# Expert rows of PEER gathered and summed in packs of 4 picks by 32 tokens, product-key search two heads at a time, a new table of ticks

## The reference

```python
scores = jnp.einsum('thpd,hpnd->thpn', qry, sub_keys).astype(jnp.float32)
top_s, top_i = lax.top_k(scores, PEER_TOPK)
cand_s = top_s[:, :, 0, :, None] + top_s[:, :, 1, None, :]
cand_i = top_i[:, :, 0, :, None] * PEER_NKEYS + top_i[:, :, 1, None, :]
...
best_s, best_pos = lax.top_k(cand_s, PEER_TOPK)
idx = jnp.take_along_axis(cand_i, best_pos, axis=-1)
gate = jax.nn.softmax(best_s, axis=-1)
u = expert_u[idx]
act = jax.nn.gelu(jnp.einsum('thkd,td->thk', u, x_blk), approximate=False)
vsel = expert_v[idx]
return jnp.einsum('thk,thkd->td', (gate * act).astype(vsel.dtype), vsel)
```

## Time and profile before

| | |
|---|---|
| median of 3 runs | 1902.19 us |
| span of the profiled execution, first to last instruction | 1833.1 us |
| what lies around the span (median less span) | 69.1 us |
| TensorE busy | 1408.6 us (77%) |
| VectorE busy | 1011.9 us (55%) |
| GpSimd busy | 1096.8 us (60%) |
| ScalarE busy | 400.6 us (22%) |
| bytes moved by DMA | 619.35 MB, mean 338 GB/s |

### The profile page before, as it was taken

The page is one execution under the profiler, slowest core; times in us unless marked ns, Lnnn a source line. Parts: engine busy times, 40 slices in busy tenths (PEclk is TensorE's granted clock), DMA queues, the critical chain, the costliest instruction groups (busy, mean ns, idle before and its releaser), DMA issues.

```text
span 1833.1 us, 14206 instructions
## 1 busy us (share of the span) xinstructions
PE 1408.6 (77%) x4217; PEld 708.3 (39%) x4217; DVE 1011.9 (55%) x2342; ACT 400.6 (22%) x1019; POOL 1096.8 (60%) x1049
## 2 busy tenths in 40 slices
PE   7988405776887896697868878867899977778886
PEld 6768402222332332245423333323564433223332
DVE  4655697774544444864595456477308355444441
ACT  5645201111211211520112102133213202111111
POOL 2010038777777675776656777557535677777772
PEclk9999757989999898898889898979999988998898
DMA  8250239999999999999988999999978899999995
GB/s 324 80 207 1 84 133 332 389 361 383 409 409 409 366 383 402 409 397 404 404 309 302 409 409 405 401 405 329 397 248 276 318 391 401 389 410 409 409 409 202
DMA packets 182515, 619.35 MB, mean 338 GB/s; under 512 B 18405, under 2 KB 18441, under 8 KB 182441
## 3 DMA queue, kind: packets, MB, share of 16 engines
q0 software_dynamic: 153568, 561.12, 79.5%
q1 hardware_dynamic: 28496, 57.28, 8.3%
q10 hardware_dynamic: 376, 0.05, 0.0%
HBM read 617.34 MB, written 1.05 MB: 337 GB/s over the span
## 4 chain that ended last, share of the span: by engine, by line
PE 30%; DMA 24%; POOL 24%; DVE 11%; issue 9%; ACT 2%; ACTq 0%; DVEq 0%
PE banks L492 19%; POOL arena L308 18%; DMA arena<-in_peer_u_dram,hnT 12%; POOL raw L308 6%; DMA arena<-in_peer_v_dram,hnT 6%; DMA raw<-in_peer_u_dram,hnT 5%; PE banks L370 3%; PE banks L376 3%; DVE arena L1309 2%; PE banks L630 1%; DVE arena L1353 1%; DVE arena L1351 1%; PE banks L516 1%; DVE raw L1309 1%; DMA arena<-in_diff_w_in_dram 1%
## 5 line engine op out<-in xcount | busy, mean ns | idle before, releaser
L492 PE MATMUL banks<-arena,hnT 128*128 128x512 f32 x2048 | 1024.7, 650 | 324.9 <-ACT hnT L851 267.8
L492 PEld LDWEIGHTS banks<-arena,hnT 128*128 128x128 f32 x2048 | 408.5, 207 | 887.5 <-issue 562.7
L308 POOL DMA_INDIRECT arena<-in_peer_v_dram,hnT x512 | 535.6, 1046 | 250.4 <-PE banks L492 143.0
L1309 DVE CUSTOM_DVE_ANT_0 raw<-raw,hrows 128x1024 f32<-128x1024 f32 x256 | 312.4, 1224 | 313.6 <-DMA raw<-in_peer_u_dram,hnT 312.6
L1309 DVE CUSTOM_DVE_ANT_0 arena<-arena,hrows 128x1024 f32<-128x1024 f32 x256 | 311.7, 1224 | 274.6 <-DMA arena<-in_peer_u_dram,hnT 274.2
L308 POOL DMA_INDIRECT raw<-in_peer_u_dram,hnT x256 | 273.1, 1067 | 255.2 <-DVE hnT L1409 140.6
L308 POOL DMA_INDIRECT arena<-in_peer_u_dram,hnT x256 | 274.3, 1071 | 110.0 <-issue 70.4
L851 ACT ACTIVATE hnT<-ident,hnT 128x128 f32<-128x128 f32 x512 | 169.7, 391 | 159.2 <-PE banks L492 119.0
L845 ACT ACTIVATE hnT<-hnT 128x8 f32<-128x8 f32 x64 | 13.4, 209 | 810.8 <-DVE hnT L1309 810.7
L516 PE MATMUL banks<-arena,work 128*128 128x512 f32 x256 | 124.3, 621 | 12.5 <-ACT work L873 6.8
L1041 DVE TENSOR_TENSOR split<-arena,split 128x512 fp32r<-128x512 f32 x96 | 63.5, 689 | 47.6 <-ACT split L716 47.2
(11 more groups left out here) (194 smaller groups left out, 708.9 us busy)
## 6 DMA issues: line engine op xcount, KB each, us to landing
arena<-in_diff_w_in_dram SPq DMA_DIRECT2D x24, 1024.0 KB, 18.1
arena<-in_peer_w_query_dram SPq DMA_DIRECT2D x16, 1024.0 KB, 13.4
arena<-in_gla_w_in_dram POOLq DMA_DIRECT2D x5, 2048.0 KB, 23.0
arena<-in_peer_w_query_dram POOLq DMA_DIRECT2D x4, 2048.0 KB, 16.6
arena<-in_peer_v_dram,hnT POOLq DMA_INDIRECT x512, 7.8
arena<-in_diff_w_out_dram SPq DMA_DIRECT2D x8, 1024.0 KB, 19.7
arena<-in_gla_w_out_dram POOLq DMA_DIRECT2D x2, 2048.0 KB, 10.9
raw<-in_peer_u_dram,hnT POOLq DMA_INDIRECT x256, 7.9
```

Of the source, the lines that this page charges most:

```text
L308: pool.indirect_dma_start(rows(n), None, table.rearrange("l e d -> (l e) d"), bass.IndirectOffsetOnAxis(ap=places[:, o:o + 1].bitcast(u32) ...
L492: last = nc.tensor.matmul(bank(2 * (tile % NT) + half), diags[:, n % BUFS * P:(n % BUFS + 1) * P], v_rows(n)[:, half * 512:(half + 1) * 51 ...
L1309: V.tensor_tensor_reduce(out=u_rows(n), in0=u_rows(n), in1=hrows[:, o // SLOTS, :], scale=1.0, scalar=0.0, op0=ALU.mult, op1=ALU.add, accu ...
```

## The change

Five things, in one diff.

1. **V rows in packs.** A V gather of before brings, for one pick, the rows of 128 tokens. Now four V gathers together bring four picks of 128 tokens in another arrangement: gather j of a pack brings the rows of tokens 32j to 32j+31, and the partition's quarter says which of the four picks it is. The number of gathers and their size stay. The list of places, the gates and the Gelus have to be rearranged for that, which ScalarE does in 16 small copies each (`packed`, on 32 partitions): per list of 32 picks for places and gates, per 8 picks for the Gelu.
2. **Sums of 32 columns.** The weight matrix of a gather is 128x32 (four stacked identities, `ident4`, scaled), and its sum writes 32 partitions of PSUM: `expert_sums` does eight matmuls of 128x32 by 128x512 for a pack of four, four next to each other into the four quarters of a bank. V buffers come free in fours.
3. **Search and lists per two heads.** `search(tile, b)` handles heads 2b and 2b+1 and sets `listed` for 32 picks; the softmax of these two heads is part of it. The order on DVE beside it is changed: between the lists of tile 2 stand steps of layer 1 of the second token group.
4. **A new table.** From tick 16 on one U and one V gather per tick, V 16 picks behind U, to tick 520 (before: 598 ticks). `START` is now 0, 128, 256, 384, `BASE` 148 and 276.
5. Key scores of layer 1 are computed block by block within the query projection, so that the first search can start earlier (`SEARCH_T` is counted from `Q_END[0]`).

```diff
+PACK = 4
+LIST = 2 * TOPK
+LISTS = SLOTS // LIST
+PACK_T = P // PACK
...
+LAG = 16
+PLAN = ((0, 0, 0), (LAG, LAG, 0), (ROWS, ROWS, ROWS - LAG), (ROWS + LAG // 2, ROWS, ROWS))
 TICKS = PLAN[-1][0]
-START = (0, 128, 280, 464)
-GATES = (0, 55, 268, 450)
-BASE = (140, 326)
-FINAL = 492
+START = (0, 128, 256, 384)
+BASE = (148, 276)
+FINAL = 430
...
-SEARCH_T = Q_END[3] + 4
+SEARCH_T, PAIR_T = Q_END[0] + 4, 15
+SEARCH = [PAIR_T * n for n in range(NT * LISTS)] + [t + SEARCH_T + PAIR_T * b for t in BASE for b in range(LISTS)]
+SEARCH[10], SEARCH[11] = BASE[1] + 2, BASE[1] + IN_END[1] + 2
...
                 for n in range(v_at(t), v_at(t + 1)):
+                    if n % LIST == 0:
+                        pool.wait_ge(S("v_listed"), n // LIST + 1)
                     if n >= BUFS:
-                        pool.wait_ge(S("v_used"), n - BUFS + 1)
-                    gather(peer_v, n, v_rows, "v_loaded")
+                        pool.wait_ge(S("v_used"), (n - BUFS) // PACK + 1)
+                    gather(peer_v, n, v_places, v_rows, "v_loaded")
...
-            def expert_sum(n):
-
-                tile = n // SLOTS
-                if n % SLOTS == 0 and tile >= NT:
+            def expert_sums(first):
+
+                tile = first // SLOTS
+                if first % SLOTS == 0 and tile >= NT:
                     pe.wait_ge(S("h_updated"), 2 * (tile - NT + 1))
-                pe.wait_ge(S("diag_ready"), n + 1)
-                pe.wait_ge(S(f"v_loaded{n % BUFS}"), 16 * (n // BUFS + 1))
+                pe.wait_ge(S("diag_ready"), first + PACK)
+                for n in range(first, first + PACK):
+                    pe.wait_ge(S(f"v_loaded{n % BUFS}"), 16 * (n // BUFS + 1))
                 for half in range(2):
-                    last = nc.tensor.matmul(bank(2 * (tile % NT) + half),
-                                            diags[:, n % BUFS * P:(n % BUFS + 1) * P],
-                                            v_rows(n)[:, half * 512:(half + 1) * 512],
-                                            start=(n % SLOTS == 0), stop=(n % SLOTS == SLOTS - 1))
+                    for j in range(PACK):
+                        n, r0 = first + j, j * PACK_T
+                        last = nc.tensor.matmul(bank(2 * (tile % NT) + half)[r0:r0 + PACK_T, :],
+                                                diags[:, n % BUFS * PACK_T:(n % BUFS + 1) * PACK_T],
+                                                v_rows(n)[:, half * 512:(half + 1) * 512],
+                                                start=(first % SLOTS == 0), stop=(first % SLOTS == SLOTS - PACK))
                 last.then_inc(S("v_used"), 1)
...
-                while summed < v_at(int(t) - SUM_LAG):
-                    expert_sum(summed)
-                    summed += 1
+                while summed + PACK <= v_at(int(t) - SUM_LAG):
+                    expert_sums(summed)
+                    summed += PACK
...
+            def packed(dst, src, function):
+
+                for s in range(PACK):
+                    to = dst[s * PACK_T:(s + 1) * PACK_T].rearrange("p (g j) -> p g j", j=PACK)
+                    for j in range(PACK):
+                        of = src[j * PACK_T:(j + 1) * PACK_T].rearrange("p (g s) -> p g s", s=PACK)
+                        last = A(to[:, :, j], of[:, :, s], function)
+                return last
...
-                A(acts[:, o], dots[:, o], ACT.Gelu).then_inc(S("gelu_done"), 1)
+                packed(acts[:, o], dots[:, o], ACT.Gelu).then_inc(S("gelu_done"), 1)
...
-                A(diags[:, n % BUFS * P:(n % BUFS + 1) * P], ident[:], ACT.Copy,
+                A(diags[:, n % BUFS * PACK_T:(n % BUFS + 1) * PACK_T], ident4[:], ACT.Copy,
                   scale=weights[:, n % PICKS:n % PICKS + 1]).then_inc(S("diag_ready"), 1)
...
-                two_rounds(HP, 350, lambda j: sc[:, j * NK:(j + 1) * NK],
+                two_rounds(4, 260, lambda j: sc[:, j * NK:(j + 1) * NK],
...
+            attended(0)
+            search(2, 0)
+            search(2, 1)
+            mix_rows(1)
+            search(2, 2)
+            turned(1, 0)
+            search(2, 3)
+            turned(1, 1)
+            attended(1)
+            for b in range(LISTS):
+                search(3, b)
```

More of the change, by code:

```diff
@@ L61, with lists_at @@
 Q_END = [Q_T + 4 * KD * Q_STEP * (b + 1) for b in range(4)]
-SEARCH_T = Q_END[3] + 4
+SEARCH_T, PAIR_T = Q_END[0] + 4, 15
+SEARCH = [PAIR_T * n for n in range(NT * LISTS)] + [t + SEARCH_T + PAIR_T * b for t in BASE for b in range(LISTS)]
+SEARCH[10], SEARCH[11] = BASE[1] + 2, BASE[1] + IN_END[1] + 2
+def lists_at(t, late, after):
+    return sum(min(SEARCH[n] + late, START[n // LISTS] + n % LISTS * LIST + after) <= t
+               for n in range(2 * NT * LISTS))
 def placed(t, which):
@@ L176, in trunk_kernel @@
         words = hnT[:].rearrange("p k t -> p (k t)")
-        dots, acts, weights, places, diags = (words[:, o:o + n] for o, n in (
-            (0, PICKS), (PICKS, PICKS), (2 * PICKS, PICKS), (3 * PICKS, PICKS), (4 * PICKS, BUFS * P)))
+        dots, acts, weights, places, v_places, gates, diags = (words[:, o:o + n] for o, n in (
+            (0, PICKS), (PICKS, PICKS), (2 * PICKS, PICKS), (3 * PICKS, PICKS), (4 * PICKS, PICKS),
+            (5 * PICKS, PICKS), (6 * PICKS, BUFS * PACK_T)))
         def x1(unit, off=0, n=D):
@@ L304, in _, with gather @@
                                    ).then_inc(S("keys_loaded"), 16)
-            def gather(table, n, rows, loaded):
+            def gather(table, n, of, rows, loaded):
                 o = n % PICKS
@@ L1331, in at, with tops, search @@
                     ticks += 1
-            def tops(off, half):
-                return ar(off, HP * TOPK).rearrange("p (h q k) -> p h q k", h=PH, q=2)[:, :, half, :]
-            def search(tile, t):
+            def tops(off, half, b):
+                return ar(off + b * 4 * TOPK, 4 * TOPK).rearrange("p (h q k) -> p h q k", h=2, q=2)[:, :, half, :]
+            def search(tile, b):
+                t = SEARCH[tile * LISTS + b]
+                at(t)
+                first = tile % NT * SLOTS + b * LIST
                 spent = 0
-                latest = START[tile]
+                latest = START[tile] + b * LIST
                 def used(ns):
@@ L1373, in search @@
+                step(V.tensor_copy(ar(tif, 4 * TOPK), ar(ti, 4 * TOPK).bitcast(u32)))
+                s1 = tops(A_TS, 0, b).unsqueeze(3).broadcast_to([P, 2, TOPK, TOPK])
+                s2 = tops(A_TS, 1, b).unsqueeze(2).broadcast_to([P, 2, TOPK, TOPK])
+                step(V.tensor_tensor(cand.rearrange("p (h a b) -> p h a b", h=2, a=TOPK), s1, s2, ALU.add))
+                used(800)
                 ordered()
-                bs, bp, gg = A_BS, A_BP, A_GG + tile % NT * SLOTS
-                two_rounds(PH, 480, lambda j: cand[:, j * 256:(j + 1) * 256],
+                bs, bp, gg = A_BS + b * LIST, A_BP + b * LIST, A_GG + first
@@ L1405, in search @@
-                    used(2300)
+                    step(V.tensor_reduce(ar(ij + half * LIST, LIST), e3, AX.X, ALU.add))
+                    used(600)
                 ordered()
-                step(V.tensor_scalar(ar(ij, SLOTS), ar(ij, SLOTS), float(NK), float(tile // NT * NEXP), ALU.mult, ALU.add))
+                step(V.tensor_scalar(ar(ij, LIST), ar(ij, LIST), float(NK), float(tile // NT * NEXP), ALU.mult, ALU.add))
                 ordered()
-                V.tensor_tensor(places[:, tile % NT * SLOTS:(tile % NT + 1) * SLOTS].bitcast(i32), ar(ij, SLOTS), ar(ij + SLOTS, SLOTS),
+                V.tensor_tensor(places[:, first:first + LIST].bitcast(i32), ar(ij, LIST), ar(ij + LIST, LIST),
@@ L1410, in search @@
                                 ALU.add).then_inc(S("listed"), 1)
[L1412 to L1416 removed]
+                sm = A_SM
+                dve.wait_ge(S("gate_exps"), tile * LISTS + b + 1)
+                step(V.tensor_reduce(ar(sm, 2), g3, AX.X, ALU.add))
```

193 lines of the change are left out of this document (101 added, 92 removed).

## The result

The changed kernel takes **1977.85 us**, the median of 4 runs (1971.25 to 1985.16), where the kernel before took 1901.68 us beside it: ratio **1.0395 [1.0361, 1.043]**. It is slower; 1821 us and a gain had been forecast. The profiled execution took 1977.94 us.

The account below looks back on a forecast made before the run. No engine was taken to bound the whole; the second half was a flow of gathers with a floor of 1.28 us each. 1626 + 33 + 5 + 30 + 12 = 1706, + 45.7 = 1752, with 69.1 gives 1821 us; range 1760 to 1890.

Parts of the forecast that it names:

- The first U gather: Start of the gather flow: a quarter of the search suffices, so it starts at 214.2 us, 40 us earlier (38 to 42).
- the rival: TensorE's 32-column sums: the columns don't overlap, a pack takes 6.9 us, 1866 us in all; chance 0.07.
- The search's 0.10 us for each gather: Search beside the dots on VectorE: lengthens each of 330 gathers by 0.10 us, 33 us in all (0 to 115).
- The sum: Whole kernel: last U gather at 1706 us plus 45.7 us of end gives 1752 us of span, 81 less than before.
- the floor: Whole kernel: dots and gathers fall into step, attention has slack, only 12 us of waits remain; 1753 us; chance 0.15.
- ScalarE. ... Nothing is added to the sum: ScalarE's Gelus of 16 instructions take 3.3 us for 0.2, 64 times; V 16 ticks behind U covers it, cost 0.
- Outside layer 1 ... no stall: V buffers outside layer 1: rows land after 7.8 us, sum 2 us, buffer needed 12.8 us behind; no stall.
- V buffers in packs: Attention of layer 1: loop of 14.0 us against 10.2, 3.8 us for each of 4 packs, twice: 30 us (0 to 60).
- half clock: TensorE: granted clock falls towards 0.50, a pack takes 4 us in 10.2; it waits for nothing there, costed at nothing.
- In the projections the weights fill such gaps: Projections of layer 1: weight loads fill the gaps from V buffer waits; hardly any waits of GpSimd for sums expected there.
- fourth rival: All of layer 1: GpSimd goes in step with TensorE, 3.8 us for each of 45 packs, 1962 us; chance 0.09.
- the 69.1 us around the span: Outside the profiled span: 69.1 us taken as time around it, added to 1752 us of span to give 1821 us.

## Why the prediction was wrong

**What held.** The first U gather starts at 214.6 us (214.2 had been worked out); its wait is ended by the first list:

```profile
L1467 DVE TENSOR_TENSOR hnT<-arena x16: 191/192/193, 214.2 to 1664.9; 128x32 int32<-128x32 f32 x16
```

Four sums of 32 columns do run side by side. At the full clock a pack is 1.92 us, where 2.0 was said and 6.9 would have been the rival. The first row stands behind an idle stretch, at a mean granted clock of 0.55, the second right behind it, at 1.00:

```profile
1612.49 3.41 PE L509 MATMUL banks<-arena,hnT 128*32 128x512 f32 x16 [17.96 <-issue]
1617.25 1.92 PE L509 MATMUL banks<-arena,hnT 128*32 128x512 f32 x16 [1.35 <-DMA arena<-in_peer_v_dram,hnT]
```

The Trainium skill (TensorEngine Tiling (Array Packing), Theoretical Speedup) gives up to 4x for 32 columns; the second row shows 6.9 / 1.92 = 3.6, and the earlier trace rows had shown only two. The search's 0.10 us for each gather is neither borne out nor refuted. With the diagonals first, 8 ticks took 21.8 us with the search beside them (picks 16 to 120), but 22.7 in the last flow without it; with SUM_LAG 2 as well they took 22.6 and 21.1. What lengthens a gather there is a dot, search or none, and the sum had counted that for the ticks with a search only. In the changed kernel itself a gather took 1.57 us in those ticks, above the 1.5 that the prediction named as a sign against it. The sum, 1752 us of span, is nearly met by the kernel without packs (1742.7), which is not the kernel it was made for, and by that with both edits (1765.0). The range began at 1760 us, above the 1753 of the floor that it was said to nearly take in.

**The step that failed first** is "ScalarE. ... Nothing is added to the sum", with its cover of 16 ticks. The 3.3 us were right (3.44). Wrong was to look at how far V stands behind U and not at what stands ahead of what in ScalarE's queue in one tick. With 16 = 2 x 8 the late Gelu and the needed diagonal meet in every group. The order of ScalarE's instructions that is shown ahead of the prediction says it: two Gelus, then seven diagonals (L898, x7) and not eight. The eighth, without which the second pack isn't whole, stands behind the third Gelu. I read there only that each Gelu had become 16 instructions. The same holds for "Outside layer 1 ... no stall": the V buffers were counted to be needed 12.8 us behind the gather, with the sum ready as soon as rows and TensorE were, and no diagonal in the count. Price on chip A: 136 us (147 by the ratios), the gain of the diagonals put first. The sentence "If the cover were gone, a pack's diagonals would be 3.3 us late and so would the V gathers" had the mechanism: 8 ticks were 25.4 - 22.7 = 2.7 us longer for it in the last flow, and over some 60 groups that is 160 us, less what loads hide.

**The step that was too small** is "V buffers in packs". For the attention it had "14.0 us where the flow needs 10.2" (its terms add up to 13.9), 4 packs, twice, 30 us. The loop is there as described, with 17.6 us in place of 14.0 and 5 or 6 packs a pass. The largest part of the error is the pack, taken at 2 us: it was written three paragraphs before that TensorE would fall to half clock and that this costs nothing, and exactly here TensorE is waited for. It is 3.64 us. With SUM_LAG 2 the loop has room again, and 68 us are gained with the diagonals first (40 of the 79 us between the two profiled spans lie in the attentions). That this lock comes of freeing V buffers in fours is shown by the kernel without packs that waits in fours. Wrong outright was "In the projections the weights fill such gaps": the fours cost 55 us in the parts of layer 1 outside the attentions, and the changed kernel waits 40.2 us for sums in one input projection alone. So the prediction's fourth rival, GpSimd in step with TensorE through all of layer 1, to which it gave 0.09, was right in its place, though not in its price. It is half of the story: against the kernel without packs on A the changed kernel loses 109 us in layer 1 (U picks 148 to 375: 840.7 and 732.0 us), but also 63 us ahead of it and 57 behind it, where the Gelu holds the diagonal.

**The step beside them** is "the 69.1 us around the span": no run has more than some 2 us there. Chip A and chip B differ by 3.3% for before (1840.81 and 1901.68 us), and by 0.1% for the changed kernel. This hid part of the error: on chip A the ratio is 1.081.

**The sum.** On chip A, from the changed kernel: 1980.17 - 136.4 (diagonals first) - 67.7 (SUM_LAG 2) = 1776.1 us, which is simply the time of the kernel with both, against 1752 + 2 forecast for a chip like it. Its profiled span is 1765.0 us: the last U gather starts at 1721.2, where 1706 had been summed, and the end takes 43.8 us, where 45.7 had been taken. I did not take the 15 us apart. It also stays open whether packs can be made to gain at all, and how the kernel without packs and with both edits stands on chip A.

## What to carry to other kernels

Where engines run through one table of ticks, write down for each in-order queue what stands directly ahead of the instruction that frees a buffer, and what that neighbour waits for; a distance in ticks is no cover when the two fall into the same tick, and swapping two loops costs nothing. Freeing buffers in fours takes slack out of every loop that goes through them, projections included, and the loop must be summed at the half clock that the saved work itself brings. And compare a span only with a time of the same execution: the chip may be another one.

## What the runs showed of the hardware

- Four float32 matmuls of 128x32 by 128x512 into the four quarters of a bank cost little more than one of 128 columns: 0.96 against 0.86 us (half of 1.92 and of 1.72). Eight of them (16 instructions) take 1.92 us at a granted clock of 1.00, the level of 2.4 GHz, and 3.41 to 3.64 us at 0.50 to 0.55, all or nearly all of it at the level of 1.2 GHz. Of the slow ones shown, three came behind 7 to 18 us of idleness and one (3.47 us) right behind such a pack; the mean granted clock of the last flow fell from 0.89 without packs to 0.61 with them (both on A).
- ScalarE takes 3.44 us for 16 pieces of 32 x 2 elements, 215 ns each; one piece of 128 x 8 took 209.
- Chips differ. Where sums held it for little, the last flow ran at 373 to 399 GB/s on chip A and at 364 to 373 on B. Ticks 16 to 148 of the kernel without packs took 353 us on A, and 388 and 389 us in its two variants on B.
- A gather that begins while a dot runs can take twice as long: with the diagonals first, the 66 gathers of the last flow that began beside no dot took 0.94 us in the mean, the 63 others 1.27, up to 1.98. It depends on the order: with SUM_LAG 2 as well, 62 began beside a dot and took 1.03.
